# Packing the rows of a TensorE operand buffer from 544 to 512 columns in a two-block transformer kernel

## The chip, the cores and the metric

The kernel runs on one core of one Trainium2 chip. The metric is the device time of one execution in microseconds, as a median over runs. The profiled execution is one further run of the same program; all rows below come from it.

## What is computed

Two transformer blocks follow each other on 256 tokens of width 2048, in float32. The part that matters here is the long row of products of the activations with weight matrices:

```python
h = rms_norm(r, g_mix[i]); z = h @ w_in[i]              # 2048 x 11264 + ...
y_attn = attn @ w_attn_out[i]; y_conv = (c_b * conv(c_c * c_x, w_conv)) @ w_conv_out[i]
r = r + (sigmoid(g_a) * y_attn + sigmoid(g_c) * y_conv) @ w_o[i]
r = r + square(relu(rms_norm(r, g_mlp) @ w_up)) @ w_down            # 8192 wide
r = r + sigmoid(rms_norm(r, g_ple) @ w_ple_gate) * (p @ w_ple_proj)
# second block, with 16 meta tokens ahead of the 256:
u = conformer_conv(rms_norm_2(h, norm_mix_pre), ...)                # 31 taps, layer norm, silu, @ w_out
h = h + rms_norm_2(u, norm_mix_post)
u = swiglu(rms_norm_2(h, norm_ffn_pre), w_gate, w_up, w_down)       # 5632 wide
h = h + rms_norm_2(u, norm_ffn_post)
```

The meta tokens matter only as the left context of the second block's convolution; the output is the 256 ordinary tokens.

## The kernel before

**Split operands.** Every float32 value is split into a high half (rounded to TensorE's fp32r format) and a low half (the remainder). A product is taken as high x high + high x low + low x high. The activations stand transposed in SBUF, in two buffers of 16 rows (`kt`, one for each 128 of the contraction): `A` has rows of 2 x 272 columns (`TM` = 272 = 16 meta tokens + 256), `B` has rows of 2 x 256. In `B` the high half of a row is columns 0 to 255 and the low half columns 256 to 511, side by side. In `A` the high half begins at column 0 and the low half at column 272, so that with 256 tokens 16 unused columns lie between the two and 16 behind the second. A row of `A` is 2176 bytes long, one of `B` 2048 bytes. Only the second block's first convolution product (`conv2`, lines 591 to 609) uses all 272 columns.

**The matmuls.** `step` (lines 379 to 413) makes one half panel: 256 output columns over one contraction. Weights come in units of 1024 columns in a ring of four slots (`stage`, loaded by SP's queue; `whi` made by ScalarE on line 735; `wlo` made by VectorE on line 1221). A unit holds 4 `kt` by 2 output tiles, which is 8 pairs. A pair is one matmul of `whi` with both halves of the row (512 columns, line 397) and one of `wlo` with the high half (256 columns, line 400). With `hi_first=True` the eight 512-column matmuls of a unit come first and the eight 256-column ones after them (line 408). 64 pairs (a `body`, two half panels) are one iteration of a phase.

**The phases** run in this order; TensorE's instructions stand in program order and nothing reorders them.

| phase | iterations of 64 pairs | reads |
|---|---|---|
| qkv | 6 (first two and last `hi_first`) | A |
| ga, ccx, first half of cb | 4 + 4 + 1, `hi_first`, attention steps between them | A |
| second half of cb, gc | 1 + 4 | A |
| attn_out, conv_out | 2 + 2 | B |
| w_o | 4 | A |
| up, down, four rounds | 4 + 4 each | B, A |
| gate | 4 | B |
| conv2 | own code, 272 columns | A |
| out2 | 4 | B |
| glu0, back0 | 8, 4 | A, B |
| glu1, back1 | 8, 4 | A, B |
| glu2, back2 | 6, 3 | A, B |

Between some phases stand other TensorE instructions: `column_sums` (lines 423 to 433, two float32 matmuls of ones with `acc`, for the RMS norms) inside the first iteration of gate and the second of glu0, and after `ple` and out2; transposes of small inputs before w_o; 16 transposes of `r` before back2 (line 680). qkv iterations 2 to 4 are ordinary, as are all phases from the second half of cb on.

**Writers of A.** ScalarE writes the high half and VectorE the low half, through `part` (line 130): for x on lines 799 and 1280, for the merged mixer output (914, 1427), the hidden layer of the first MLP (970, 1483), the normed input of the second block (935, 1270, with `meta=META`, in the 272-column form) and of the last MLP (1135, 1152, 1626, 1631). The meta tokens' columns are written on lines 993 and 1850.

Of the kernel before, what the change touches and what calls it, by code (L numbers as in the profile page):

```python
# [24 lines left out]
F32 = mybir.dt.float32  # L25
F32R = mybir.dt.float32r
ALU = mybir.AluOpType
ACT = mybir.ActivationFunctionType
AX_X = mybir.AxisListType.X
ds = bass.ds  # L30

P = 128
D = 2048
T = 256
KT = D // P
# [6 lines left out]
TM = T + META  # L42
# [39 lines left out]

def two_block_kernel(nc, io, out):
    at, _, UNITS = plan()

    with ExitStack() as ctx:
        def sb(name, shape, dt=F32, where=ctx):
            return where.enter_context(nc.sbuf_tensor(name, shape, dt))

        def sem(name):  # L90
            return ctx.enter_context(nc.semaphore(name))
# [3 lines left out]
        A = sb("A", [P, KT, 2 * TM], F32R)  # L95
# [3 lines left out]
        wlo = sb("wlo", [P, RING, UNIT], F32R)  # L99
# [24 lines left out]
        gp = ctx.enter_context(nc.psum_tensor("gp", [P, 4, 512], F32))  # L124
# [2 lines left out]
        ones = ones_r[:].bitcast(F32)  # L127
        sq_parts = B[:, KT - 2:KT, :]

        def part(M, which, i, n, meta=0):  # L130

            a = which * (TM if M is A else T) + meta
            return M[:, i:i + n, a:a + T] if isinstance(i, int) else M[:, ds(i, n), a:a + T]

        def both_parts(M, kt):

            return M[:, kt, :].rearrange("p (a t) -> p a t", a=2)[:, :, 0:T]

        def x_home(c):

            return [xp[:, 2:4, :], gp[:, 2:4, :], xp[:, 0:2, :], xp[:, 2:4, :]][c].rearrange("p a (b t) -> p (a b) t", b=2)
# [61 lines left out]
        def col(name, i):  # L203

            half, c = vec[name]
            return gv[:, half, ds(c + i, 1)]
# [8 lines left out]
        x_turned, x_hi, h1_ready = sem("x_turned"), sem("x_hi"), sem("h1_ready")  # L215
# [162 lines left out]
        def _(pe):  # L378
            def step(hp, j, n0, M, kt0=0, units=4, slot0=0, ready=None, after=None, single=False, hi_first=False, mid=None):

                for u in range(units):
                    slot = (slot0 + u) % RING
                    pe.wait_ge(hi_ready if hi_first else lo_ready, n0 + u + 1)
                    if u == 0 and not (isinstance(hp, int) and hp == 0):
                        pe.wait_ge(evacuated, XSLOTS + hp - 1)
                    for k in range(4):
                        if single and u == 0 and k < 2:
                            pe.wait_ge(ready[0], ready[1] + k + 1)
                        elif ready and k % 2 == 0:
                            pe.wait_ge(ready[0], ready[1] + ready[2] * u + ready[2] // 2 * (k // 2 + 1))  # L390
                        kt = kt0 + 4 * u + k
                        first, last = u == 0 and k == 0, u == units - 1 and k == 3
                        for m in range(2):
                            c = k * HPW + m * P
                            hi, lo = whi[:, slot, c:c + P], wlo[:, slot, c:c + P]
                            bank = gp[:, 2 * j + m, :]
                            nc.tensor.matmul(bank.rearrange("p (a t) -> p a t", a=2), hi, both_parts(M, kt),  # L397
                                             start=first, stop=False)
                            if not hi_first:
                                done = nc.tensor.matmul(bank[:, T:2 * T], lo, M[:, kt, 0:T], start=False, stop=last)  # L400
                    if mid and u in mid:
                        mid[u]()
                    if hi_first:
                        pe.wait_ge(lo_ready, n0 + u + 1)
                        for k in range(4):
                            for m in range(2):
                                c = k * HPW + m * P
                                done = nc.tensor.matmul(gp[:, 2 * j + m, T:2 * T], wlo[:, slot, c:c + P], M[:, kt0 + 4 * u + k, 0:T],  # L408
                                                        start=False, stop=u == units - 1 and k == 3)
                    done.then_inc(unit_used, 1)  # L410
                    if after and u in after:
                        for f in after[u]:
                            f()
# [109 lines left out]
            for k in range(KT):  # L523
                done = nc.tensor.transpose(xp[:, 3, k * TAPS2:(k + 1) * TAPS2], taps_raw[:, k * P:k * P + P],
                                           ident[0:TAPS2, 0:TAPS2])
# [24 lines left out]
            for k in range(KT):  # L550
                done = nc.tensor.transpose(xp[:, 2, k * META:(k + 1) * META], meta_raw[:, k * P:k * P + P],
                                           ident[0:META, 0:META])
# [9 lines left out]
            for u in range(4):  # L562
                pe.wait_ge(lo_ready, n0 + u + 1)
                for j in range(2):
# [5 lines left out]
                    for m in range(2):  # L570
                        o = gp[:, pair % 4, m * T:m * T + T]
                        for k in range(2):
                            c = k * 512 + (2 * j + m) * P
                            nc.tensor.matmul(o, whi[:, u, c:c + P], pT[:, k, 0:T], start=(k == 0), stop=False)  # L574
                            nc.tensor.matmul(o, whi[:, u, c:c + P], pT[:, k, T:2 * T], start=False, stop=False)
                            done = nc.tensor.matmul(o, wlo[:, u, c:c + P], pT[:, k, 0:T], start=False, stop=(k == 1))
# [71 lines left out]
            for a in range(PE_LAST):  # L648
                t = DVE_LAST + a
                done = nc.tensor.matmul(xp[:, 3, 0:T], diag_last[:, a, :], cin2[:, KT - 1, t:t + T],  # L650
                                        start=(a == 0), stop=(a == PE_LAST - 1))
# [56 lines left out]
            for part_of in range(2):  # L708
# [3 lines left out]
                for t in range(2):  # L712
                    for m in range(2):
                        done = nc.tensor.matmul(gp[:, 3, 2 * t + part_of:2 * t + part_of + 1], src[:, m * T + t * P:m * T + t * P + P],
                                                ones_r[:, 0:1].bitcast(F32), start=(m == 0), stop=(m == 1))
# [13 lines left out]
        def _(act):  # L729
# [66 lines left out]
            def hi_of_x(c, half):  # L796
                act.wait_ge(x_turned, 2 * c + half + 1)
                for kk in (2 * half, 2 * half + 1):
                    nc.scalar.activation(A[:, 4 * c + kk, 0:T], x_home(c)[:, kk, :], ACT.Copy,
                                         scale=col("g_mix", 4 * c + kk)).then_inc(x_hi, 1)  # L800

            def copy_x(c):
# [114 lines left out]
            for phase, tail in (("attn_out", attn_out_tail), ("conv_out", conv_out_tail)):  # L917
                hp0, n0 = at[phase]
                with act.Fori(0, 2) as it:
                    for j in range(4):  # L920
                        n = n0 + 8 * it + 2 * j
# [74 lines left out]
            n, q, hp0 = at["gate"][1] + 24, at["gate"][1] // RING + 6, at["gate"][0]  # L996
# [3 lines left out]
            n, q = n + 4, q + 1  # L1000
# [87 lines left out]
            for c in range(8):  # L1088
# [3 lines left out]
                for m in range(2):  # L1092
                    kt = 2 * c + m
# [19 lines left out]
            n, q = n0 + 24, n0 // RING + 6  # L1113
# [3 lines left out]
            n, q = n + 4, q + 1  # L1117
# [99 lines left out]
        def _(dve):  # L1217
# [58 lines left out]
            for c in range(4):  # L1276
                for kk in range(4):
                    kt = 4 * c + kk
                    dve.wait_ge(x_hi, 4 * c + 2 * (kk // 2) + 2)
                    nc.vector.scalar_tensor_tensor(A[:, kt, TM:TM + T], x_home(c)[:, kk, :], col("g_mix", kt),  # L1280
                                                   A[:, kt, 0:T].bitcast(F32), ALU.mult, ALU.subtract).then_inc(h1_ready, 1)
                take_lo(c, c)

            def normed_into(dst, ready):
# [225 lines left out]
            n = at["gate"][1] + 24  # L1510
# [58 lines left out]
            last = gp[:, 0, :]  # L1569
# [399 lines left out]
```

## Time and profile before

| | us |
|---|---|
| median of 3 runs (2576.67 to 2580.68) | 2580.13 |
| the profiled execution | 2578.83 |
| its span, first to last instruction | 2577.0 |
| TensorE busy in the span | 2539.5 |
| VectorE busy | 1747.1 |
| ScalarE busy | 1274.8 |
| GpSimd busy | 460.4 |

The execution's time is 1.83 us more than its span. TensorE's matmuls overlap each other in the record (the next one starts before the modelled end of the one before), so that the durations of single matmuls do not add up to the busy time. What a pair costs is read from start to start.

### The profile page before, as it was taken

To read this page: it belongs to the slowest core of one execution; us is meant where nothing else is said; L and a number is where in the kernel's file an instruction comes from. 1 tells how busy PE (TensorE), PEld (TensorE's weight loads), DVE (VectorE), ACT (ScalarE), POOL (GpSimd) and SP (SyncE) were. 2 spreads that over 40 slices of the span, in tenths; PEclk is the share of its full clock that TensorE was granted. 3 is DMA by queue.
4 is the path that set the end of the run, shared out by engine and by line. 5 is a ranking of instruction groups with operands and counts; after the bars stand their busy time and mean duration, and the time that the engine had idled before them with its cause. 6 is when DMAs were issued, how large, how long until landed. Compare 5 with 4: busy or idle time off the path is not lost.

```text
span 2577.0 us, 43865 instructions
## 1 busy us (share of the span) xinstructions
PE 2539.5 (99%) x14995; PEld 2247.8 (87%) x14995; DVE 1747.1 (68%) x2112; ACT 1274.8 (49%) x1604; POOL 460.4 (18%) x300
## 2 busy tenths in 40 slices
PE   9999999999999999999999999989899999999998
PEld 7888788888888888888888899978788888888887
DVE  6578875677765665665667789984766556665665
ACT  5456555554544444444445554455644444444444
POOL 4034410001100000000011278862400000000003
PEclk9999999999999999999999999999999999999999
DMA  6655456665566566666655665536465556666653
GB/s 210 200 170 177 147 180 196 189 192 179 189 189 190 182 195 188 188 190 188 191 186 173 192 168 163 163 107 188 145 191 187 187 179 188 195 191 190 188 180 131
DMA packets 497408, 465.28 MB, mean 181 GB/s; under 512 B 14475, under 2 KB 494213, under 8 KB 497285
## 3 DMA queue, kind: packets, MB, share of 16 engines
q1 hardware_dynamic: 496816, 463.92, 58.1%
q8 instruction: 43, 0.70, 0.1%
q10 hardware_dynamic: 516, 0.38, 0.1%
q14 instruction: 33, 0.27, 0.0%
HBM read 462.15 MB, written 2.10 MB: 180 GB/s over the span
## 4 chain that ended last, share of the span: by engine, by line
PE 93%; DVE 4%; ACT 1%; issue 1%; DMA 1%; DVEq 0%; ACTq 0%; POOL 0%; POOLq 0%; SPq 0%
PE gp L397 55%; PE gp L400 26%; PE gp L408 2%; PE gp L606 2%; PE gp L604 2%; PE gp L605 2%; DVE wlo L1221 1%; DMA stage<-in_w_in 1%; PE xp L622 0%; ACT whi L735 0%; DVE xp L1550 0%; PE xp L650 0%; DVE root L1255 0%; DVE A L1280 0%; PE gp L574 0%
## 5 line engine op out<-in xcount | busy, mean ns | idle before, releaser
L1221 DVE TENSOR_TENSOR wlo<-stage,whi 128x1024 fp32r<-128x1024 f32 x811 | 1015.9, 1268 | 679.5 <-ACT whi L735 672.7
L735 ACT ACTIVATE whi<-stage 128x1024 fp32r<-128x1024 f32 x876 | 916.2, 1057 | 952.9 <-PE gp L400 733.2
L397 PE MATMUL gp<-A,whi 128*128 128x512 f32 x3968 | 1314.2, 393 | 10.6 <-DVE A L1631 7.0
L400 PE MATMUL gp<-A,wlo 128*128 128x256 f32 x3200 | 898.2, 281 | 0.0
L397 PEld LDWEIGHTS gp<-A,whi 128*128 128x128 f32 x3968 | 739.3, 188 | 174.9 <-issue 10.6
L397 PE MATMUL gp<-B,whi 128*128 128x512 f32 x2496 | 873.4, 395 | 9.8 <-DVE B L1601 7.9
L400 PE MATMUL gp<-B,wlo 128*128 128x256 f32 x2496 | 699.5, 280 | 0.0
L400 PEld LDWEIGHTS gp<-A,wlo 128*128 128x128 f32 x3200 | 603.8, 189 | 0.0
L397 PEld LDWEIGHTS gp<-B,whi 128*128 128x128 f32 x2496 | 468.5, 188 | 118.7 <-issue 10.8
L400 PEld LDWEIGHTS gp<-B,wlo 128*128 128x128 f32 x2496 | 472.2, 189 | 0.0
L1769 POOL TENSOR_TENSOR sq<-r 128x512 f32 (+1 forms) x32 | 39.9, 1245 | 812.2 <-DVE r L1453 756.2
L1550 DVE SCALAR_TENSOR_TENSOR xp<-work,taps,xp 128x256 f32<-128x256 f32 x405 | 163.9, 481 | 2.6 <-PE xp L622 2.6
L1858 POOL TENSOR_TENSOR wlo<-stage,whi 128x1024 fp32r<-128x1024 f32 x65 | 156.0, 2405 | 38.5 <-ACT whi L735 37.9
L604 PE MATMUL gp<-A,whi 128*128 128x272 f32 x512 | 150.7, 294 | 0.0
L1769 POOL TENSOR_TENSOR sq<-work 128x512 f32<-128x512 f32 x14 | 15.5, 1106 | 747.3 <-DVE work L1687 685.5
L606 PE MATMUL gp<-A,wlo 128*128 128x272 f32 x512 | 147.7, 288 | 0.0
L605 PE MATMUL gp<-A,whi 128*128 128x272 f32 x512 | 147.3, 288 | 0.0
L748 ACT ACTIVATE cross<-gp 128x512 f32<-128x512 f32 x203 | 118.0, 581 | 3.2 <-PE gp L400 3.2
L408 PEld LDWEIGHTS gp<-A,wlo 128*128 128x128 f32 x768 | 102.8, 188 | 12.5 <-DVE wlo L1221 4.3
L1232 DVE TENSOR_TENSOR s<-gp,cross 128x512 f32<-128x512 f32 x165 | 112.8, 683 | 1.2 <-ACT cross L748 0.9
L408 PE MATMUL gp<-A,wlo 128*128 128x256 f32 x768 | 106.0, 280 | 3.0 <-DVE wlo L1221 3.0
L605 PEld LDWEIGHTS gp<-A,whi 128*128 128x128 f32 x512 | 97.1, 190 | 0.5
(294 smaller groups left out, 1428.6 us busy)
## 6 DMA issues: line engine op xcount, KB each, us to landing
stage<-in_w_in SPq DMA_DIRECT2D x160, 512.0 KB, 4.6
stage<-in_w_up SPq DMA_DIRECT2D x128, 512.0 KB, 3.8
stage<-in_w_down SPq DMA_DIRECT2D x128, 512.0 KB, 4.3
stage<-in_ffn_w_gate SPq DMA_DIRECT2D x88, 512.0 KB, 4.5
stage<-in_ffn_w_up SPq DMA_DIRECT2D x88, 512.0 KB, 4.5
stage<-in_ffn_w_down SPq DMA_DIRECT2D x88, 512.0 KB, 4.3
stage<-in_conv_w_in SPq DMA_DIRECT2D x64, 512.0 KB, 4.0
stage<-in_w_o SPq DMA_DIRECT2D x32, 512.0 KB, 4.4
```

The costliest lines, as they stand in the source:

```text
L397: nc.tensor.matmul(bank.rearrange("p (a t) -> p a t", a=2), hi, both_parts(M, kt), start=first, stop=False)
L400: done = nc.tensor.matmul(bank[:, T:2 * T], lo, M[:, kt, 0:T], start=False, stop=last)
L408: done = nc.tensor.matmul(gp[:, 2 * j + m, T:2 * T], wlo[:, slot, c:c + P], M[:, kt0 + 4 * u + k, 0:T], start=False, stop=u == units - 1 a ...
L604: nc.tensor.matmul(o, hi, A[:, kt, 0:TM], start=first, stop=False)
L605: nc.tensor.matmul(o, hi, A[:, kt, TM:2 * TM], start=False, stop=False)
L606: done = nc.tensor.matmul(o, lo, A[:, kt, 0:TM], start=False, stop=last)
L735: nc.scalar.activation(whi[:, slot, :], stage[:, slot, :], ACT.Copy).then_inc(hi_ready, 1)
L748: nc.scalar.activation(cross[:], gp[:, 2 * j:2 * j + 2, T:2 * T], ACT.Copy).then_inc(cross_out, 1)
L1221: nc.vector.tensor_tensor(wlo[:, slot, :], stage[:, slot, :], whi[:, slot, :].bitcast(F32), ALU.subtract).then_inc(lo_ready, 1)
L1232: nc.vector.tensor_tensor(dst, gp[:, 2 * j:2 * j + 2, 0:T], cross[:], ALU.add).then_inc(evacuated, 1)
L1550: nc.vector.scalar_tensor_tensor(V[:, i, :] if t == last_odd else o, x, w, o, ALU.mult, ALU.add).then_inc(tap_done, 1)
L1858: nc.gpsimd.tensor_tensor(wlo[:, slot, :], stage[:, slot, :], whi[:, slot, :].bitcast(F32), ALU.subtract).then_inc(lo_ready, 1)
```

## The change

The 16 rows that are read and written with 256 tokens are no longer those of `A` but of a view `A_packed` on the first 8192 columns of the same memory: 16 rows of 512 columns, high half at column 0 and low half at column 256, as in `B`. `conv2`, and the writers with `meta=META` that feed it, keep the rows of 544. All instructions stay, in number, order, shape and with their waits.

```diff
+        A_packed = A[:].rearrange("p k t -> p (k t)")[:, 0:KT * 2 * T].rearrange("p (k t) -> p k t", k=KT)
+
+        def packed(M):
+            return A_packed if M is A else M
+
         def part(M, which, i, n, meta=0):
-            a = which * (TM if M is A else T) + meta
-            return M[:, i:i + n, a:a + T] if isinstance(i, int) else M[:, ds(i, n), a:a + T]
+            a = which * (TM if meta else T) + meta
+            rows = packed(M) if not meta else M
+            return rows[:, i:i + n, a:a + T] if isinstance(i, int) else rows[:, ds(i, n), a:a + T]
 
         def both_parts(M, kt):
-            return M[:, kt, :].rearrange("p (a t) -> p a t", a=2)[:, :, 0:T]
+            return packed(M)[:, kt, :].rearrange("p (a t) -> p a t", a=2)
...
-                                done = nc.tensor.matmul(bank[:, T:2 * T], lo, M[:, kt, 0:T], start=False, stop=last)
+                                done = nc.tensor.matmul(bank[:, T:2 * T], lo, packed(M)[:, kt, 0:T], start=False, stop=last)
...
-                                done = nc.tensor.matmul(gp[:, 2 * j + m, T:2 * T], wlo[:, slot, c:c + P], M[:, kt0 + 4 * u + k, 0:T],
+                                done = nc.tensor.matmul(gp[:, 2 * j + m, T:2 * T], wlo[:, slot, c:c + P], packed(M)[:, kt0 + 4 * u + k, 0:T],
...
-                    nc.scalar.activation(A[:, 4 * c + kk, 0:T], x_home(c)[:, kk, :], ACT.Copy,
+                    nc.scalar.activation(A_packed[:, 4 * c + kk, 0:T], x_home(c)[:, kk, :], ACT.Copy,
...
-                    nc.vector.scalar_tensor_tensor(A[:, kt, TM:TM + T], x_home(c)[:, kk, :], col("g_mix", kt),
-                                                   A[:, kt, 0:T].bitcast(F32), ALU.mult, ALU.subtract).then_inc(h1_ready, 1)
+                    nc.vector.scalar_tensor_tensor(A_packed[:, kt, T:2 * T], x_home(c)[:, kk, :], col("g_mix", kt),
+                                                   A_packed[:, kt, 0:T].bitcast(F32), ALU.mult, ALU.subtract).then_inc(h1_ready, 1)
```

## Rows read from the trace of the kernel before

**Rows 1.** The page: span, busy time, TensorE's granted clock in 40 slices

```profile
span 2577.0 us, 43865 instructions
...
PE 2539.5 (99%) x14995; PEld 2247.8 (87%) x14995; DVE 1747.1 (68%) x2112; ACT 1274.8 (49%) x1604; POOL 460.4 (18%) x300
...
PEclk9999999999999999999999999999999999999999
```

**Rows 2.** The chain that ended last, shares by line

```profile
PE gp L397 55%; PE gp L400 26%; PE gp L408 2%; PE gp L606 2%; PE gp L604 2%; PE gp L605 2%; DVE wlo L1221 1%; DMA stage<-in_w_in 1%; PE xp L622 0%; ACT whi L735 0%; DVE xp L1550 0%; PE xp L650 0%; DVE root L1255 0%; DVE A L1280 0%; PE gp L574 0%
```

**Rows 3.** Groups by line and shape: the 512-column matmuls, and two VectorE writers

```profile
L397 PE MATMUL gp<-A,whi 128*128 128x512 f32 x3968 | 1314.2, 393 | 10.6 <-DVE A L1631 7.0 <-DVE A L1280 2.6 <-DVE wlo L1221 0.6
...
L397 PE MATMUL gp<-B,whi 128*128 128x512 f32 x2496 | 873.4, 395 | 9.8 <-DVE B L1601 7.9 <-DVE wlo L1221 1.2 <-issue 0.7
...
L408 PE MATMUL gp<-A,wlo 128*128 128x256 f32 x768 | 106.0, 280 | 3.0 <-DVE wlo L1221 3.0
...
L1483 DVE TENSOR_TENSOR A<-s,A 128x512 f32 x32 | 22.2, 692 | 32.8 <-ACT A L970 32.8
...
L1662 DVE TENSOR_TENSOR B<-s,B 128x512 f32 x20 | 13.8, 692 | 18.8 <-ACT B L1165 18.8
```

**Rows 4.** Timeline (start, length): first matmuls of up0, down0, up1, down1

```profile
682.39 0.47 PE L397 MATMUL gp<-B,whi 128*128 128x512 f32 x1 [0.69 <-issue]
...
771.22 0.39 PE L397 MATMUL gp<-A,whi 128*128 128x512 f32 x1
...
860.39 0.39 PE L397 MATMUL gp<-B,whi 128*128 128x512 f32 x1
...
949.13 0.39 PE L397 MATMUL gp<-A,whi 128*128 128x512 f32 x1
```

**Rows 5.** Timeline: glu0 from its column sums on, then the starts of back0, glu1, back1, glu2

```profile
1849.86 0.59 PE L427 MATMUL xp<-acc,ones_r 128*128 128x256 f32 x2
...
1850.64 0.39 PE L397 MATMUL gp<-A,whi 128*128 128x512 f32 x1
...
2001.49 0.40 PE L397 MATMUL gp<-B,whi 128*128 128x512 f32 x1
...
2091.94 0.40 PE L397 MATMUL gp<-A,whi 128*128 128x512 f32 x1
...
2270.30 0.39 PE L397 MATMUL gp<-B,whi 128*128 128x512 f32 x1
...
2359.05 0.39 PE L397 MATMUL gp<-A,whi 128*128 128x512 f32 x1
```

**Rows 6.** Timeline: gate after its column sums, to its one idle, and to conv2

```profile
1402.90 0.59 PE L427 MATMUL xp<-acc,ones_r 128*128 128x256 f32 x2
...
1403.68 0.40 PE L397 MATMUL gp<-B,whi 128*128 128x512 f32 x1
...
1439.72 0.40 PE L397 MATMUL gp<-B,whi 128*128 128x512 f32 x1
...
1441.43 0.47 PE L397 MATMUL gp<-B,whi 128*128 128x512 f32 x1 [1.19 <-DVE wlo L1221]
...
1485.88 0.29 PE L604 MATMUL gp<-A,whi 128*128 128x272 f32 x1
```

**Rows 7.** Timeline: the transposes after glu2, the start and the end of back2

```profile
2492.81 1.91 PE L680 MATMUL xp<-ident,r 128*128 128x128 f32 x16
...
2494.47 0.48 PE L397 MATMUL gp<-B,whi 128*128 128x512 f32 x1
...
2562.40 0.71 PE L680 MATMUL xp<-ident,r 128*128 128x128 f32 x5
```

**Rows 8.** Timeline: one unit of a hi_first iteration

```profile
132.33 2.02 PE L397 MATMUL gp<-A,whi 128*128 128x512 f32 x8
134.18 1.10 PE L408 MATMUL gp<-A,wlo 128*128 128x256 f32 x8
```

## The prediction

> **What bounds the kernel now.** I read the page first: TensorE is busy for 2539.5 of 2577.0 us, at full granted clock in every slice, the next engine for 1747.1 [rows 1]. The chain that ended last says the same with lines: 55% of the span is line 397 and 26% line 400 [rows 2]. The groups by line then show how little TensorE waits: 10.6 us ahead of the matmuls that read `A` and 9.8 ahead of those that read `B` [rows 3]. So the time is the sum of start-to-start intervals of TensorE, and a change that touches no count, no order and no wait can act through the length of these intervals alone. The mean durations do not help: 393 ns for 512 columns from `A`, 395 from `B` [rows 3], and they would say that the rows of `A` are the better ones. They include overlap and stretches at other speeds. I went to the timeline and divided the distance from the start of one phase to that of the next by its pairs.
>
> **What a pair costs in each layout.** Down0 reads `A`: 860.39 - 771.22 = 89.17 us for 256 pairs, 348.3 ns. Up1 reads `B`: 949.13 - 860.39 = 88.74 us, 346.6 ns [rows 4]. The same slots, banks and loops; only the operand differs. So packed rows look 1.7 ns a pair cheaper. But that is one of two speeds of `B`. Back0: 2091.94 - 2001.49 = 90.45 us for 256 pairs, 353.3 ns. Back1, the same code: 2359.05 - 2270.30 = 88.75 us, 346.7 [rows 5]. `A` has two speeds as well, closer together: glu0 after its column sums takes 2001.49 - 1850.64 = 150.85 us for 431 pairs, 350.0 ns; glu1 takes 2270.30 - 2091.94 = 178.36 us for 512 pairs, 348.4 [rows 5]. I call them fast and slow. In numbers: `A` 348.3 or 350.0, packed 346.6 or 353.3.
>
> **What sets the speed.** Gate shows a switch in both directions. Behind the float32 matmuls of the column sums, with no idle time, it goes on at (1439.72 - 1403.68) / 102 pairs = 353.3 ns. Then comes an idle of 1.19 us, and the last 128 pairs take 1485.88 - 1441.43 = 44.45 us, 347.3 with the cost of restarting in it [rows 6]. Back2 starts directly behind the transposes of `r`: 67.93 us for 192 pairs, 353.8 [rows 7]. Up0 starts after 0.69 us of idle and runs fast: 88.83 us, 347.0 with its restart [rows 4]. So a speed is taken at a disturbance and kept until the next one, across hundreds of pairs. No semaphore wait or transfer explains it, as no idle stands between the pairs. Two more rows of the pattern matter. Back0 follows glu0's slow 350.0 with nothing between them and is slow. Glu1 follows the slow back0, also with nothing between them, and is fast [rows 5]. I read this as: rows of `A` let the pipeline fall out of the slow pattern, and packed rows do not. That reading rests on one transition.
>
> **The change part by part.**
> No instruction is added or removed. The writers: VectorE's subtraction into `A` takes 692 ns for 512 elements a partition, that into `B` 692 [rows 3]; nothing to gain or lose, and VectorE has 830 us of slack [rows 1]. `conv2` keeps its layout: 0.
>
> Reads, ordinary pairs. There are 3968 matmuls of line 397 on `A`, of which 768 belong to `hi_first` [rows 3], so 3200 ordinary pairs. Fast to fast is 346.6 - 348.3 = -1.7 ns, fast to slow +5.0, slow to slow +3.3.
> - Down, 1024 pairs: each round follows an up phase that reads `B` and is fast, with nothing between. Fast: -1.7 us. I am sure of this one.
> - qkv 2 to 4 (192 pairs), half of cb and gc (320), w_o (256), the start of glu0 (80): 848 pairs. Fast to fast -1.4 us in all. Slow: w_o +1.3, qkv +1.0, cb and gc +1.6, and behind gc the 256 pairs of attn_out and conv_out, fast now, would go along at 6.7 ns each, +1.7. The trace has no packed phase that enters as these do. I take fast and keep the other end.
> - Glu0 behind its column sums, 432 pairs. The instructions ahead of it are those of gate [rows 5, 6], where packed rows came out slow. Slow: 432 x 3.3 = +1.4 us. Back0 is slow already: 0. Then what now cures the slow pattern, the rows of `A` in glu1, is gone. Slow glu1: 512 x 4.9 = +2.5. Slow back1: 256 x 6.7 = +1.7. Slow glu2: 384 x 5.0 = +1.9. Back2 has its own entry and stays. Sum +7.5 us.
>
> Reads, `hi_first`, 768 pairs. A unit takes some 1.85 us for its eight 512-column matmuls (134.18 - 132.33) [rows 8], 231 ns each. No row shows packed rows in this order. The gain is bounded by the 1.7 ns of an ordinary pair, 768 x 1.7 = 1.3 us, the loss by the 5.0 ns of the slow pattern, 3.8 us. I take -1.0, near the first, since the attention steps between the units disturb the order so often that no pattern should hold for long.
>
> The sum: -1.7 - 1.4 - 1.0 + 7.5 = +3.4 us. Against the profiled execution, 2578.8 becomes 2582.2; against the median of 2580.1, which is 1.3 us above it, 2583.5.
>
> The Trainium skill, Advanced Engine Details and Errata, section SBUF Cachelines, says that SBUF reads run at full performance as long as at least two accesses fall on one 16-byte line. Both layouts read runs of 1024 bytes and more, so by that rule they would cost the same, and the sum would be 0. The trace does not agree: 348.3 against 346.6 ns [rows 4], a small difference but one of whole phases.
>
> **The rivals.**
> (a) Fast everywhere. Glu0 comes out of its column sums fast, since it does not enter them exactly as gate does. Then glu0 gains 432 x 3.4 = 1.5 us, back0, which follows, 256 x 6.7 = 1.7, glu1 0.9 and glu2 0.6. With the other terms, -4.1 - 4.7 = -8.8 us: 2571.3, 0.34% faster. For it: packed rows are fast in up0, up1, back1 and the rest of gate [rows 4, 5, 6]. Against it: of the three entries behind float32 work without idle that I could place, gate and back2 were slow on packed rows and glu0 was slow on `A` [rows 5, 6, 7].
> (b) Slower. Besides the last MLP, w_o and the stretch from cb to conv_out take the slow pattern at their entries. It decides at one place above all, the switch from `hi_first` to ordinary pairs in cb, behind which 576 pairs run without a pause: 320 x 5.0 + 256 x 6.7 = +3.3 against -0.5. With w_o (+1.3 against -0.4) the sum is 3.4 + 3.8 + 1.7 = +8.9 us: 2589.0. With qkv and `hi_first` at their upper bounds as well (+1.3 and +4.8 more) it is 2595. From +5.2 us on it counts as slower, which the cb entry alone brings about.
> (c) No effect. The 1.7 ns come from something other than the layout, such as where `B` lies, and the slow pattern of packed rows does not arise in `A`'s memory. 2580. The transition rows speak against it; the rule of the page above, cited there, gives this result.
> (d) The slow pattern ends by itself or at some small disturbance in glu1. Then +1.4 stands and most of the rest falls: about 2577 to 2579, no difference. I count it with (c).
>
> **How the numbers follow.** The slow last MLP with the rest fast: 0.33, 2583.5. (a) 0.29. (b) 0.23. (c) with (d) 0.15. The three runs of before lie within 4 us, which is as much as two or three phases changing their speed by chance, so each case has about 2 us on either side. The range takes in (a), 2571.3 less its scatter, and (b) to its middle value with scatter: 2570 to 2591. The likeliest case has its own range of 2580 to 2587. A difference under 0.2%, 5.2 us, is about what a measurement of this kernel cannot tell from no change. Faster by more: nearly all of (a), 0.28. Slower by more: (b) and the upper edge of the likeliest case, 0.27. Within: 0.45.
>
> **What would show it.** In the timeline of the changed kernel, the distances between phase starts: down1 88.7 us (not 89.2) confirms the fast price. Glu1 180.9 us (slow, 353.3) or 177.5 (fast, 346.6) decides between the forecast and (a); back1 90.4 or 88.7 goes with it. Gc to conv_out and w_o show (b). If glu1 keeps 178.4 and down1 89.2, it is (c). The forecast is wrong if glu0 leaves its column sums at 346.6, or if a slow stretch heals on packed rows without any idle. A changed idle time ahead of lines 397 or 400 would mean that the cause lies outside what I looked at.

## The result, and the profile after

The changed kernel takes 2590.39 us as the median of 20 runs (2577.97 to 2603.63), the kernel before 2578.98 (2574.63 to 2583.95). The ratio is 1.0042 with a 95% interval of 1.0033 to 1.0051: slower, by 11.4 us between the medians. The profiled execution has a span of 2588.6 us, 11.6 more than before.

The 20 times of the changed kernel are not one cluster. Three lie at 2578.0 to 2580.5, sixteen at 2588.3 to 2593.4, one at 2603.6. Those of before form one group 9.3 us wide. This will matter below.

The page of the kernel after, to be read against [rows 1]:

```profile
span 2588.6 us, 43865 instructions
...
PE 2550.5 (99%) x14995; PEld 2246.0 (87%) x14995; DVE 1747.4 (68%) x2112; ACT 1274.8 (49%) x1604; POOL 460.8 (18%) x300
```

The same instructions, the same clock, and TensorE is busy for 11.0 us longer. The rest of its span, in which it is idle, went from 37.5 to 38.1 us. Its longest wait, for the writer of `B`, is 7.9 us as before [rows 3], and the second, for the writer of `A` in glu0, went from 7.0 to 6.9. (Line 397 is line 404 now.) So nearly all of the time is in the intervals between matmuls. The timeline of the kernel after at the starts of phases (start, length, line):

```profile
377.10 0.48 PE L404 MATMUL gp<-A,whi 128*128 128x512 f32 x1
...
493.06 0.40 PE L404 MATMUL gp<-B,whi 128*128 128x512 f32 x1
...
583.51 0.27 PE L556 MATMUL xp<-ident,work 128*128 128x128 f32 x1
...
585.13 0.50 PE L404 MATMUL gp<-A,whi 128*128 128x512 f32 x1
...
675.68 0.29 PE L565 MATMUL xp<-work,ones_r 128*128 128x16 f32 x2
...
778.15 0.39 PE L404 MATMUL gp<-A,whi 128*128 128x512 f32 x1
...
866.90 0.39 PE L404 MATMUL gp<-B,whi 128*128 128x512 f32 x1
...
1855.03 0.59 PE L434 MATMUL xp<-acc,ones_r 128*128 128x256 f32 x2
...
2008.10 0.40 PE L404 MATMUL gp<-B,whi 128*128 128x512 f32 x1
...
2098.55 0.40 PE L404 MATMUL gp<-A,whi 128*128 128x512 f32 x1
...
2279.46 0.40 PE L404 MATMUL gp<-B,whi 128*128 128x512 f32 x1
...
2369.91 0.40 PE L404 MATMUL gp<-A,whi 128*128 128x512 f32 x1
...
2507.25 0.48 PE L404 MATMUL gp<-B,whi 128*128 128x512 f32 x1
...
2573.90 0.27 PE L687 MATMUL xp<-ident,r 128*128 128x128 f32 x1
```

And the rows of the kernel before that answer to the first five and are not ahead of the prediction:

```profile
374.65 0.48 PE L397 MATMUL gp<-A,whi 128*128 128x512 f32 x1
...
489.00 0.39 PE L397 MATMUL gp<-B,whi 128*128 128x512 f32 x1
...
577.75 0.27 PE L549 MATMUL xp<-ident,work 128*128 128x128 f32 x1
...
579.37 0.50 PE L397 MATMUL gp<-A,whi 128*128 128x512 f32 x1
...
668.65 0.29 PE L558 MATMUL xp<-work,ones_r 128*128 128x16 f32 x2
```

Subtracting neighbouring starts gives the whole account:

| stretch | before us | after us | difference |
|---|---|---|---|
| start to the last attention step, in cb (qkv, `hi_first`) | 374.65 | 377.10 | +2.45 |
| rest of cb, gc | 114.35 | 115.96 | +1.61 |
| attn_out, conv_out (`B`) | 88.75 | 90.45 | +1.70 |
| w_o | 89.28 | 90.55 | +1.27 |
| down, four rounds | 4 x 89.17 | 4 x 88.75 | -1.68 |
| glu0 from its column sums on | 151.63 | 153.07 | +1.44 |
| back0 (`B`) | 90.45 | 90.45 | 0 |
| glu1 | 178.36 | 180.91 | +2.55 |
| back1 (`B`) | 88.75 | 90.45 | +1.70 |
| glu2 with the transposes behind it | 135.42 | 137.34 | +1.92 |
| back2 (`B`) | 67.93 | 66.65 | -1.28 |

The sum is +11.7 us, against +11.6 of the span. Two of the rows that lose, attn_out with conv_out and back1, do not read the changed buffer at all.

The first row of the table needs a closer look, since more than half of it does not come from the layout. Qkv's first ordinary pair starts at 61.03 us before and at 62.55 after, so 1.52 of the 2.45 us are lost by then. The chain that ended last (start, length) shows one transfer of weights there, in the kernel before and in the kernel after:

```profile
41.87 14.04 DMA stage<-in_w_in
...
41.99 15.45 DMA stage<-in_w_in
```

It took 1.4 us longer in the one profile. In two kernels further down that have the old rows up to this point (packed rows only in down, and the one built on a map), the same pair starts at 65.40 and 62.26 us. So this part is scatter between executions. From there the 192 ordinary pairs of qkv cost 69.41 us instead of 68.48, which is +0.93, and the `hi_first` units behind them cost nothing: the first of them starts at

```profile
129.51 2.03 PE L397 MATMUL gp<-A,whi 128*128 128x512 f32 x8
...
131.96 2.03 PE L404 MATMUL gp<-A,whi 128*128 128x512 f32 x8
```

before and after, and the distance to the last attention step (374.65, 377.10) is 245.14 us in both.

### The profile page after: what moved, and what is told of

Same layout as the page of the kernel before. It is cut to its first block, busy times and chain, and to the rows that moved or that the text cites. A ratio compares the mean times of both kernels' runs of the same rounds, so it can differ in the third digit from the quotient of the medians.

```text
span 2588.6 us, 43865 instructions
## 1 busy us (share of the span) xinstructions
PE 2550.5 (99%) x14995; PEld 2246.0 (87%) x14995; DVE 1747.4 (68%) x2112; ACT 1274.8 (49%) x1604; POOL 460.8 (18%) x300
## 4 chain that ended last, share of the span: by engine, by line
PE 92%; DVE 4%; ACT 1%; issue 1%; DMA 1%; DVEq 0%; ACTq 0%; SPq 0%
PE gp L404 55%; PE gp L407 25%; PE gp L415 2%; PE gp L613 2%; PE gp L611 2%; PE gp L612 2%; DVE wlo L1228 1%; DMA stage<-in_w_in 1%; PE xp L629 0%; ACT whi L742 0%; DVE xp L1557 0%; PE xp L657 0%; DVE root L1262 0%; DMA work<-in_x 0%; DVE A L1287 0%
```

## Experiments

Each was run beside the kernel before on the same chip. Two theories are under test. The lock theory is that of the prediction: on packed rows TensorE keeps one of two patterns, 346.7 or 353.3 ns a pair, from one disturbance to the next. Its rival, the place theory, says that the speed belongs to a phase and what the other engines and the DMA do beside it.

**Which property of the old rows ends the slow pattern?** Two kernels change one property each of the packed rows.

```diff
-        A_packed = A[:].rearrange("p k t -> p (k t)")[:, 0:KT * 2 * T].rearrange("p (k t) -> p k t", k=KT)
+        A_packed = A[:, :, 0:2 * T]
```

> The rows of A keep their distance of 544 columns (2176 bytes), but the low half lies directly behind the high half, as in packed rows. If the row distance is what releases the slow pattern (odd rows begin at an odd multiple of 128 bytes), glu1 takes 348.3 ns a pair as before, 178.4 us, the span is near 2577, and gc to conv_out goes back to 88.8 us. If it is the gap of 16 columns between the halves that does it, glu1 stays at 353.3 ns, 180.9 us, and the span near 2588.

```diff
-        A_packed = A[:].rearrange("p k t -> p (k t)")[:, 0:KT * 2 * T].rearrange("p (k t) -> p k t", k=KT)
+        A_halves = A[:].rearrange("p k t -> p (k t)")[:, 0:KT * 2 * T].rearrange("p (a k t) -> p a k t", a=2, k=KT)
...
-            return packed(M)[:, kt, :].rearrange("p (a t) -> p a t", a=2)
+            return A_halves[:, :, kt, :] if M is A else M[:, kt, :].rearrange("p (a t) -> p a t", a=2)
```

> The 16 high halves lie first (rows of 1024 bytes) and the 16 low halves behind them, 16 KB further. Each 512-column read is two runs of 1024 bytes, as before the change, but every run begins at a multiple of 256 bytes, as after it. If the row distance and start address matter, the phases on A show the two speeds of packed rows, 346.7 and 353.3 ns a pair, span 2580 to 2590. If two runs in one read matter, they show 348.3.

Timeline of the first, with adjacent halves in rows of 544: the starts of back0, glu1, back1.

```profile
2012.98 0.40 PE L404 MATMUL gp<-B,whi 128*128 128x512 f32 x1
...
2103.43 0.40 PE L404 MATMUL gp<-A,whi 128*128 128x512 f32 x1
...
2282.64 0.40 PE L404 MATMUL gp<-B,whi 128*128 128x512 f32 x1
```

Timeline of the second, with the halves 16 KB apart: down0, up1, then glu1, back1.

```profile
780.26 0.40 PE L410 MATMUL gp<-A,whi 128*128 128x512 f32 x1
...
870.71 0.40 PE L410 MATMUL gp<-B,whi 128*128 128x512 f32 x1
...
2106.69 0.39 PE L410 MATMUL gp<-A,whi 128*128 128x512 f32 x1
...
2284.19 0.39 PE L410 MATMUL gp<-B,whi 128*128 128x512 f32 x1
```

With adjacent halves glu1 takes 179.21 us for 512 pairs, 350.0 ns, and the down phases 89.61 us for 256 each, again 350.0. That is neither 348.3 nor 353.3: it is the slow speed that the old rows had in glu0 [rows 5]. Back0 ahead of glu1 runs at 353.3 (90.45 us), and so does back1 behind it. Both expectations missed. With the halves apart down0 takes 90.45 us (353.3) and glu1 177.50 (346.7): the two speeds of packed rows, though every 512-column read is two runs, as expected of the start address (the span, 2590.3, is just above the range given). Each kernel ran once (2593.53 and 2592.07 us).

What do these two show of the end of the slow pattern? That pattern is a cycle of three pairs of 350, 361 and 349 ns by the trace's start times, so a slow phase can hand over to the next in three slots. In the kernel before, the last pair of back0 is the long one, and glu1 on the old rows is fast from its first pairs on (348.8 ns over the first 32). With packed rows the run with doubled first matmuls, further down, hands over from back0 to glu1 in the same slot and stays slow, and the changed kernel does so in another slot. That is the like-for-like comparison of the two layouts. With the halves apart the slow pattern passes from up to down in all three slots and never ends, so a read in two runs alone does not end it. With adjacent halves in rows of 544 it passed into `A` six times, each time behind the 349 ns pair and never behind the long one. So this run does not show that the row distance alone is without effect. The old rows had the distance, the split read and a low half that begins at an odd multiple of 64 bytes. Which of these ends the pattern, and in which slots, stays open. Nor do the old rows end it always: in the kernel before glu0 kept its 350.0 ns for all 431 pairs and handed the slow pattern to back0.

These two runs showed something that the prediction had taken as safe: up0 can be entered slow, and then all eight phases of up and down stay slow.

**Does a disturbance change the speed inside a phase?** The changed kernel with extra matmuls of ones between iterations of the last MLP:

```diff
+            def nudge(n):
+                nc.tensor.matmul(xp[:, 3, 0:n], ones_r[:], A_packed[:, 0, 0:n], start=True, stop=True)
...
+            run("glu1", 0, 2, A, (r_ready, 48, 4), 512)
+            run("glu1", 2, 4, A, (r_ready, 48, 4), 48)
+            run("glu1", 4, 6, A, (r_ready, 48, 4), 96)
+            run("glu1", 6, 8, A, (r_ready, 48, 4), 192)
```

> The changed kernel with one more matmul of ones (32 to 512 columns, result unused) at 13 places of the last MLP, between iterations, nothing else changed. If the speed is a pattern taken at a disturbance and kept (the lock theory), some of the stretches between two nudges run at 346.7 ns a pair and others at 353.3, each constant from its nudge to the next; from the entries seen so far I expect about half of them fast, and the span shorter by about 4 us in spite of 13 times 0.05 to 0.25 us. If the speed belongs to the phase or to what the other engines and the DMA do beside it (the place theory), glu1, back1 and glu2 stay at 353.3 throughout and the span grows by 1 to 3 us.

Timeline: glu1's four stretches of 128 pairs, from its first nudge to that of back1.

```profile
2100.76 0.39 PE L675 MATMUL xp<-A,ones_r 128*128 128x512 f32 x1
...
2145.38 0.19 PE L675 MATMUL xp<-A,ones_r 128*128 128x48 f32 x1
...
2189.87 0.21 PE L675 MATMUL xp<-A,ones_r 128*128 128x96 f32 x1
...
2235.21 0.25 PE L675 MATMUL xp<-A,ones_r 128*128 128x192 f32 x1
...
2280.54 0.22 PE L675 MATMUL xp<-A,ones_r 128*128 128x128 f32 x1
```

The distances are 44.62, 44.49, 45.34 and 45.33 us. A stretch of 128 pairs is 44.4 at the fast and 45.2 at the slow speed, and the nudge adds the rest, so glu1 ran fast, fast, slow, slow. The phase, the code and the transfers are the same in all four. In all, five of the 13 nudged stretches were fast, and the speed was constant within each. This ends the place theory. Five of 13 is fewer than the half that I expected, and the span was 2590.3 us, not about 4 us shorter than the 2588.6 of the changed kernel. Each nudge cost 0.10 to 0.24 us.

**Can a nudge hold the fast pattern?** One nudge ahead of every iteration of 64 pairs in w_o, up, down and the last MLP, with 48, 64 or 512 columns:

```diff
                     with pe.Fori(0, 4) as it:
+                        nudge(64)
```

> The changed kernel with one extra matmul of 48 columns (ones times ones, unused) ahead of every iteration of 64 pairs in w_o, up, down, and the last MLP from glu0's third iteration on. Lock theory: each iteration runs wholly at 346.7 or wholly at 353.3 ns a pair, and what follows a nudge depends on what stood before it; if 48 columns keep a fast pattern fast and sometimes turn a slow one, nearly all iterations end up fast and the span falls to 2575 or below, in spite of 66 nudges at 0.03 to 0.09 us. Place theory: the phases keep the speeds that they had in the changed kernel, and the span grows by the nudges' 2 to 6 us.

> The same with 64 columns, which turned slow to fast in both places where they were tried. Lock theory: mostly fast if 64 columns also keep a fast pattern fast (2575 or below); if they turn it back, the iterations alternate and the span is near 2585. Place theory: as for 48 columns.

> The same with 512 columns (of an unused operand, and not in w_o), which turned slow to fast once. A nudge costs 0.2 us here, 12 us for all, so the span is 2585 to 2600; what counts is which iterations are fast. Lock theory: the speed still changes only at nudges. Place theory: never.

Timeline with 64 columns: nudges of three iterations in a row.

```profile
755.84 0.19 PE L424 MATMUL xp<-ones_r 128*128 128x64 f32 x1
...
778.15 0.19 PE L424 MATMUL xp<-ones_r 128*128 128x64 f32 x1
...
800.87 0.19 PE L424 MATMUL xp<-ones_r 128*128 128x64 f32 x1
```

They are 22.31 and 22.72 us apart, a fast iteration of 64 pairs and a slow one. From 710 us to gate the iterations strictly alternated between slow and fast, and in the last MLP all were slow: 2601.52 us. With 48 columns every nudged iteration was slow: 2609.47 (there are 64 nudges, not 66). My hope for it, nearly all fast, was wrong. With 512 columns:

```profile
733.70 0.40 PE L424 MATMUL xp<-pT,ones_r 128*128 128x512 f32 x1
...
756.13 0.40 PE L424 MATMUL xp<-pT,ones_r 128*128 128x512 f32 x1
```

The iteration between these two takes 22.43 us, fast; the one ahead of them, from 710.86 on, took 22.84, slow. Every later one up to gate was fast, as was every one of the last MLP from its first nudge on. The nudges cost 0.23 us each and ate that gain: 2592.55 us. Inside each of these stretches the outcome repeats from nudge to nudge, over some 30 iterations, so it is not drawn anew each time. It does not hang on "slow" or "fast" alone, though: the 64-column nudge turned slow into fast in up and down and left it slow in the last MLP. The runs below show what else counts.

**Undoing one part: old rows in the last MLP.**

```diff
-            body("glu0", 0, A, (r_ready, 48, 4), single=True)
+            body("glu0", 0, A_wide, (r_ready, 48, 4), single=True)
...
+        def wide(which, i, n):
+            return A[:, i:i + n, which * TM:which * TM + T]
```

> The changed kernel with the old rows of 544 columns in the last MLP alone (glu0, glu1, glu2 and the writers of their operand). By the lock theory glu1 runs at 348.3 ns (178.4 us instead of 180.9), back1 at 346.7 (88.75 instead of 90.45), glu2 at 348.3 (133.8 instead of 135.7), glu0 at 350 (151.4 instead of 152.8); with back2 slow again (+1.3) the sum is -6.3 us against the changed kernel's profile, 2582.3 for the span, and +0.2% against the kernel before. If the loss were spread over all phases that read packed rows, it would give back half of the 11.6 us or less in the last MLP and nothing in back1.

Timeline: the starts of glu1 and back1.

```profile
2093.51 0.39 PE L410 MATMUL gp<-A,whi 128*128 128x512 f32 x1
...
2271.85 0.39 PE L410 MATMUL gp<-B,whi 128*128 128x512 f32 x1
```

Glu1 takes 178.34 us, as forecast, and back1 88.75. But glu0 left its column sums fast here (348.3 ns) and back0 took 88.75 us too, better than forecast. So this profile puts back the old price of the last MLP; it has no slow pattern that the old rows could have ended. The profiled span is 2578.6, against 2582.3 expected. In the 12 runs the times fall into two groups: seven at 2579.4 to 2583.2, five at 2594.5 to 2599.9. The median is 2583.16, the ratio 1.0039 (1.0021 to 1.0056). The middle of the lower group, 2582.4, is 8.0 us below the changed kernel's median. The middle of the upper one, 2595.8, is 13.3 above that. This fits what up and down cost when they are entered slow: eight phases at 1.7 us are 13.6. No run of the upper group was profiled.

**One part alone: packed rows only in down.** The kernel before, with the hidden layer's rows packed:

```diff
-                for phase, M, ready in (("up0", B, (r_ready, 0, 4)), ("down0", A, (hidden_ready, 8 * rnd, 2))):
+                for phase, M, ready in (("up0", B, (r_ready, 0, 4)), ("down0", A_packed, (hidden_ready, 8 * rnd, 2))):
```

> The kernel before with packed rows in the down phases alone (one part of the change). By the lock theory the up and down phases, all on packed rows, share one fate from up0's entry to gate: when up0 enters fast, down takes 88.75 us a round instead of 89.17 and the time is 1.7 us lower than before, 2578; when it enters slow, all eight phases take 90.45 us, 13.6 us more than when fast, 2591. In the runs with the changed rows there (changed kernel, old rows in the last MLP) 6 of 32 lay about 13 us above the others. So the runs fall into two groups 13 to 14 us apart, with most in the lower one, while those of the kernel before form one group, since the old rows of down0 end a slow pattern of up0. If old rows do nothing of the kind, the kernel before would show two groups as well. By the place theory there is one group at 2578.

Timeline: the starts of back0, glu1 and back1, on the old rows.

```profile
2003.45 0.40 PE L403 MATMUL gp<-B,whi 128*128 128x512 f32 x1
...
2093.90 0.40 PE L403 MATMUL gp<-A,whi 128*128 128x512 f32 x1
...
2272.26 0.39 PE L403 MATMUL gp<-B,whi 128*128 128x512 f32 x1
```

In the profiled execution down0 is fast, 88.75 us. Its time is 2580.91, with a start that was 4.4 us late (qkv's first ordinary pair at 65.40 us); the four others are 2590.48 to 2591.86. The median is 2590.92 against 2578.78, ratio 1.0047 (1.0034 to 1.0060). Two groups, as expected, but most runs in the upper one and the step between them some 10 us. The 1.7 us that the rows of down save by themselves show in the profile, and four runs of five lose 10 us against it. The kernel before has no such group in any of its runs. That fits old rows that end a slow up0 in down0, but the four upper runs were not profiled, and no profile shows such an end there. What the rows above show is the end of a slow back0 in glu1 a second time: 90.45 us, then 178.36 as in [rows 5]. It comes in the same slot as in the kernel before.

**Using the order of the two matmuls, at no cost.** In the first row of each half panel, 512, 512, 256, 256 columns in place of 512, 256, 512, 256:

> The changed kernel with another order at the first row of every half panel of the ordinary phases: both 512-column matmuls, then both 256-column ones, instead of 512, 256, 512, 256; no work is added. The nudges of 512 columns turned the slow pattern to fast and then kept it, and here two 512-column matmuls stand behind each other every 32 pairs in the same way. If that adjacency is what turns it, the phases on packed rows go to 346.7 ns within one or two half panels and the span falls to about 2572. If the two 256-column matmuls behind it undo it, or the extra length mattered, slow stretches remain, and the span stays between 2580 and 2590.

Timeline: the starts of two half panels in a row.

```profile
712.42 0.40 PE L405 MATMUL gp<-B,whi 128*128 128x512 f32 x1
...
723.51 0.40 PE L405 MATMUL gp<-B,whi 128*128 128x512 f32 x1
```

The third starts at 734.81. The half panels of 32 pairs take 11.09 and 11.30 us, fast and slow, and so it alternates through up, down and the last MLP. The expected fast lock did not come; the span is 2589.5.

**Doubling a real matmul.** The first 512-column matmul of a half panel is issued twice; the second starts the sum anew.

```diff
+                            if twice and first and m == 0:
+                                nc.tensor.matmul(bank.rearrange("p (a t) -> p a t", a=2), hi, both_parts(M, kt),
+                                                 start=True, stop=True)
```

> The changed kernel with the first 512-column matmul of a half panel issued twice (the second one starts the sum anew, so the result stays) at 12 places: behind each entry that can leave the slow pattern (qkv, cb, gc, w_o, up, gate, out2, glu0, back2). Cost 12 x 0.23 = 2.8 us. By the lock theory it holds about 350 or less on average in all ordinary phases: against the changed kernel's profile -12.3 us in the last MLP up to back1 and glu2, -3.8 from cb to conv_out if the two places there suffice, -1.7 in w_o, -1.7 in out2, -0.9 in qkv, less one or two that fail, so the span is 2571 to 2576 and the time is faster than before by 0.1 to 0.3%. By the place theory the span is 2591.

> The changed kernel with the first 512-column matmul of an iteration issued twice at 14 places, always 64 pairs apart as in the run with 512-column nudges at every iteration, where at most two were needed: cb, gc 0 and 1; w_o 0 and 1; up0 0, 1 and 2; gate 1; out2 1 and 2; glu0 2, 3 and 4. Cost 14 x 0.23 = 3.2 us. Lock theory: from the third place on each stretch is fast; 11.6 us back in the last MLP, about 3 from gc to conv_out, 1 each in w_o and out2, so 2577 for the median against 2590 of the changed kernel, within 0.2% of the kernel before, and no group of runs 13 us above. If the distance of the doubled matmuls is not what made them work, the last MLP stays slow in part of the runs.

The two expectations are those of this run and of a second one, with 14 such doublings always 64 pairs apart. Both missed. (The first has 11 places, not 12.) They took 2593.87 us (ratio 1.0046, 1.0024 to 1.0069) and 2592.94 (1.0057, 1.0040 to 1.0075), each with single runs from 2579 to 2608. The last MLP stayed slow in both profiles. The misses were useful. Timeline of the second, around its doubling (line 405) at glu0's third iteration:

```profile
1871.81 0.40 PE L407 MATMUL gp<-A,whi 128*128 128x512 f32 x1
...
1872.16 0.40 PE L407 MATMUL gp<-A,whi 128*128 128x512 f32 x1
...
1872.52 0.40 PE L405 MATMUL gp<-A,whi 128*128 128x512 f32 x1
```

The slow pattern is the cycle of three pairs, 350, 361 and 349 ns. Here the pair directly ahead of the doubling is the long one (0.36 us), and the pattern stays slow. Of the 25 doublings in the two profiles five stand at an entry. Three stand on a slow pattern where the long pair is due next, and all three made it fast. Eleven stand in the two other slots, and all eleven left it slow. Of six on a fast pattern five left it fast. The sixth, in out2, met another form of the fast pattern, pairs of 350 and 343 ns in turn, and made it slow. A miss also moves the slots. With 64 pairs between places each of the two misses led into the other: behind the long pair, then behind the 349 ns pair, and again, at all three places of glu0.

**A kernel built on that map.** The kernel before, with packed rows in down and the last MLP, and doublings in up0 and glu0 whose distances (32, then 96 pairs) catch both kinds of miss:

```diff
+            for it, twice in ((0, (1,)), (1, (0,)), (2, (1,)), (3, ())):
+                body("up0", it, B, (r_ready, 0, 4), twice=twice)
...
+            for it, twice in ((2, (0, 1)), (3, ()), (4, (0,))):
+                body("glu0", it, A_packed, (r_ready, 48, 4), twice=twice)
```

> The kernel before with packed rows in down and in the last MLP only, and a doubled first matmul at three places each in up0 (iterations 0, 1, 2) and glu0 (iterations 2 and 4). The 14 doublings of the run with spaced nudges and the 11 of the run with doubled first matmuls show that a slow pattern, which repeats every three pairs, ends when the doubled matmul stands behind the pair of 233 + 117 ns, and not behind the pair of 241 + 120 or that of 236 + 113; a doubling in the wrong place moves the slots, so that doublings 64 pairs apart miss for ever. The places are chosen by that: the second one 32 pairs behind the first catches one of the two misses, the third one 96 pairs later the other. Lock theory with this map: up, down, glu, back0 and back1 run at 346.7 ns from the third place on in every run, the runs form one group, the span is 2577.0 - 1.7 (down) - 1.5 (glu0) - 1.7 (back0) - 1.5 (glu1, glu2) + 1.4 (doublings) + up to 1.0 (slow until the last place) = 2573, the time 0.15% below the kernel before. If the map does not hold, there are groups 12 to 14 us apart and the median lies at 2580 or higher.

Timeline: up0's second doubling (line 405).

```profile
705.81 0.40 PE L407 MATMUL gp<-B,whi 128*128 128x512 f32 x1
...
706.17 0.40 PE L407 MATMUL gp<-B,whi 128*128 128x512 f32 x1
...
706.52 0.40 PE L407 MATMUL gp<-B,whi 128*128 128x512 f32 x1
...
706.87 0.40 PE L405 MATMUL gp<-B,whi 128*128 128x512 f32 x1
707.11 0.40 PE L407 MATMUL gp<-B,whi 128*128 128x512 f32 x1
...
707.46 0.39 PE L407 MATMUL gp<-B,whi 128*128 128x512 f32 x1
```

The first doubling had met the 350 and 343 form in up0 and turned it slow. At the second one the long pair (0.36 us) lies three pairs back and is due again, and the pairs behind it are 0.35 us each and stay so. In glu0 the first doubling hit. Glu1 and back1 in the same profile:

```profile
2089.17 0.39 PE L407 MATMUL gp<-A,whi 128*128 128x512 f32 x1
...
2266.66 0.39 PE L407 MATMUL gp<-B,whi 128*128 128x512 f32 x1
```

Back0 88.75, glu1 177.49 and back1 88.75 us: all at 346.7 ns. This is a test of the map on new places: two doublings where the long pair was due, both hits; three on the fast pattern, all kept; one on the 350 and 343 form, which turned slow as in out2. The span is 2573.1, forecast 2573. To agree so closely took luck: the start came 2.6 us late by the last attention step, and out2, where nothing was changed, happened to be 0.8 us shorter than before. The 11 times lie between 2573.05 and 2578.36 in one group, median 2574.42 against 2579.36 for the kernel before: ratio 0.9982, 0.9973 to 0.9991. It is faster than both kernels of this study.

## Why the prediction was right or wrong

**Right: the bound and the currency.** Nothing but start-to-start intervals changed; waits and writers stayed (the writer of the hidden layer's low half takes 692 ns in both). The four speeds and their persistence held to 0.1 ns: down at 346.7, glu1 at 353.3, 180.9 us as written down beforehand.

**Right: the last MLP.** Forecast +7.5 us, measured +1.44 + 2.55 + 1.70 + 1.92 = +7.6. The cause rests on two profiles in which the old rows of glu1 end a slow back0 ([rows 5], and packed rows in down only) and on three profiles with packed rows and no extra matmul there in which a slow back0 is handed on, once in the very same slot. The slow exit from the column sums was less certain than the rest: of nine profiles with packed or halves-apart rows in glu0, seven left them slow and two fast. Down was forecast at -1.7 and measured -1.68 in the profile. The statement "I am sure of this one" was too strong, though: it holds for a fast up0 alone. Up0 was entered slow in three of the nine profiles with no extra or swapped matmul at its start, and in the two of these without a doubling behind it all eight phases stayed slow. I left that case out of the account. That the old rows of down0 end it is an inference from the times alone. Of 20 runs of the changed kernel one (2603.63) lies where that case would put it.

**Wrong step: "I take fast and keep the other end".** The likeliest case had qkv, cb and gc, and w_o fast, at -1.4 us. All of them were entered slow in the profile, and attn_out with conv_out went along. From the middle of cb to the end of w_o the kernel lost 1.61 + 1.70 + 1.27 = +4.6 us. This was no chance of one profile. All seven kernels with packed or halves-apart rows there and no extra matmul at the entry of cb ran cb and gc at 353.3 ns, and all three with the old rows at 348.3; the entry of w_o was slow in all six that have it unaltered. This is rival (b), with its named mechanism at its named place: its 2589.0 for the median compares with 2590.4 measured, while the likeliest case's 2583.5 is 7 us short and its own range of 2580 to 2587 did not hold the time. The wide range of 2570 to 2591 did, at its upper edge. The evidence for the better choice was there: gate and back2 gave slow entries on packed rows [rows 6, 7], so did out2 behind its wait of 7.9 us (353.3 ns), and I let "no row shows it" stand for fast.

**Wrong reading: what an idle does.** Gate's idle of 1.19 us and up0's of 0.69 were followed by the fast speed [rows 4, 6], and I read the first as a cure. In the eleven profiles without a doubling or a swap in gate, that idle (1.19 to 1.93 us) was followed by the fast speed six times and by the slow one five times, at the same code and rows. So the speed behind such a wait is open each time, and that is probably what makes the groups in the times.

**Wrong size: `hi_first` and the start.** I took -1.0 for `hi_first`. Behind qkv it measured 0 (245.14 us in both), and up to 57.4 us, with its first two iterations, the kernel lost 0.2. The eight 512-column matmuls of a unit take 1.85 us before [rows 8] and 1.84 in the same unit after, but the eight 256-column ones took as much more, so that a unit costs 2.79 us in both. Qkv's ordinary pairs, taken as -0.3, were slow, +0.93. The remaining 1.3 us of the first row are the late weights, which no term of mine held and which the layout does not cause.

**Not foreseen: back2** gained 1.28 us. I had written that it "has its own entry and stays". Its entry is the same code, but glu2 now ends in the slow pattern, and the transposes behind it led into the fast one. Over all profiles, a fast glu2 was followed by a slow back2 seven times in seven, and a glu2 at 353.3 by a fast back2 four times in five. By the letter, my sign of being wrong (a slow stretch that heals on packed rows without any idle) was met here: TensorE does not idle between glu2 and back2, only other matmuls stand there.

**Rival (a)**, fast everywhere in the last MLP, is probably the group of three runs at 2578 to 2580.5. They lie about 12 us below the bulk, and a last MLP that gains the 4.7 us of rival (a) in place of losing 7.6 would be 12.3 below. They were not profiled, so this is an inference from times.

**The cacheline rule.** The Trainium skill, Advanced Engine Details and Errata, section SBUF Cachelines, would have both layouts cost the same. The trace does not agree: 348.3 against 346.7 ns for the old and the packed rows in down, and 350.0 with adjacent halves in rows of 544, where that rule sees no difference. The runs do not contradict what it says of strides inside a line; they show an effect of another kind beside it.

## What to carry to other kernels

When one engine is busy nearly all the time (99% of the span here), compare its start-to-start interval for the same code in different phases before and after an edit. If one code has two speeds, ask what ends the slower one, since a layout that is faster in its good state can cost more by keeping the bad one alive, and the phases that lose need not touch the edited buffer. Plot the single times as well: two groups in them are a sign of such a choice, and a median over them hides both. When a part is put back to test a cause, look in the profile whether the state that it is to act on was there at all. A gain of a fraction of a percent that depends on such a pattern is to be built with the entry under control, not only with the layout.

## What the runs showed of the hardware that was not expected

A steady stream of alternating 512- and 256-column matmuls on packed fp32r operands at the full clock has stable patterns: pairs of 346.7 ns each (or 350 and 343 in turn), and a cycle of 350, 361 and 349 ns, mean 353.3. Each survives phase changes and other operand buffers; the fast one of the changed kernel lasted from up0 to gate, 689 to 1408 us. A single extra matmul, at a cost of 0.10 to 0.24 us, can switch it. For a doubled 512-column matmul on the slow pattern the slot of the cycle decided the outcome in all 16 cases of three profiles: five of five ended the pattern where the long pair was due, and none of eleven elsewhere. For the nudges of ones the slots were not worked out. Rows of 544 columns with the halves apart run at 348.3 or 350.0, the same rows with the halves adjacent at 350.0 in the one run. What inside the chip makes the cycle of three stays open.
